# Stores of the experts' outputs in a two-block Trainium2 kernel: from one DMA a unit to one DMA a column block of four units

## The chip, the cores and the metric

The kernel runs on one core of one Trainium2 chip. The metric is the device time in microseconds (us) of one execution; the median of three runs of the kernel before is 2355.97 us (2354.79 to 2361.44).

The core has a matrix engine (PE, whose weight loads are listed as PEld), a vector engine (DVE), a scalar engine (ACT), GpSimd (POOL), and a sequencer without arithmetic (SP) that issues most DMAs. Sixteen DMA engines move data between the large memory (DRAM) and the on-chip memory of 128 partitions.

## The reference, cut to what matters

Two transformer-like blocks run on 1024 tokens of 1024 channels in float32. The first one ends in a mixture of experts, the part that the change touches: each token picks one of 4 groups and in it 2 of 8 experts, so there are 2048 assignments to 32 experts.

```
g_prob = softmax(h @ w_group + b_group);  p_g, g_idx = top_k(g_prob, 1)
top_v, top_i = top_k(logits of the experts in that group, 2)
gate = p_g * softmax(top_v);  expert_id = g_idx * 8 + top_i
def expert_block(args):
    xb, e = args
    a_, b_ = split(xb @ w13[e], 2)          # w13[e]: 1024 x 1024
    return (silu(a_) * b_) @ w2[e]          # w2[e]: 512 x 1024
out = segment_sum(ys * row_w[:, None], row_tok)
x = x + g2 * out
```

## The kernel before

The stages run one after the other: input projection and mixers of the first block, routing (`route`), the experts (`experts`, the stage "moe"), `middle` (adds the weighted expert outputs to x, then the second block's projection), attention, and a feed-forward part.

**Units and groups.** In `experts` the assignments are sorted by expert and cut into units of 32 tokens (TOK) of one expert. There are 80 of them, and four (CT) make a group of 128 rows, so 20 groups. An expert has between one and ten units.

**Weights.** An expert's weights are six pairs of 1 MB (two tiles of 128 rows by 1024). SP loads them by DMA into a ring of 17 places, `raw` (named moew_raw in the profile, L1607). A load into a place waits until the last unit of the expert that held it has copied it (`s_copied`), and until the load before with the same pair number has landed. For every unit DVE and ACT copy its expert's pairs from the ring into the working tiles: `wup`, which uses the memory of x (x_res in the profile, L1570), and `wdown` (L1581). So an expert with three units is loaded once and copied three times.

**A unit's computation.** PE computes `up` (L1673): 32 tokens as weights, four blocks of the expert's columns in four quarters of the array, into `hu`. ACT applies silu (L1714), DVE multiplies by the other half (L1768), PE transposes the result (`turn_a`, L1662), ACT copies it (L1718), and PE computes `down` (L1684) into `yp`. There partition 32 j + t holds token t of the unit and column block j of 256 columns. PE runs `down` of a unit after `up` of the next one, with `turn_a` in the middle of that `up`.

**The output.** DVE copies `yp` to `ysb` (`y_out`, L1773), a slice of acc_sq by the unit's place u in its group. ACT stores it to `y_scratch` in DRAM (`send`, L1722). Both happen two units late: at step u the output of unit u-2. A slice is written again one group later, after its store has landed (`s_sent`). The routing's row numbers `slots` let `middle` gather the outputs by token (L1851).

**Tokens.** For each group GpSimd gathers 128 token rows into `xg`, PE transposes them (L1656), and ACT and DVE write them, scaled, to `xt` (L1594, L1592).

**What sets the order.** It is written out by hand: each engine's program has a body `group` of four steps, one for each u, in a loop. Within an engine everything runs in that order; between engines semaphores count. At the end of the stage SP loads x back from `xt_scratch` (L1622), ACT waits for all stores, and all engines meet before `middle` starts.

Of the kernel before, what the change touches and what calls it, by code (L numbers as in the profile page):

```python
# [21 lines left out]
P = 128  # L22
T = 1024
D = 1024
KT = D // P
# [12 lines left out]
TOK = 32  # L38
CT = P // TOK
# [5 lines left out]
FW, YW = FF // CT, D // CT  # L45
# [218 lines left out]
class Kernel:  # L264
# [1268 lines left out]
    def experts(self):  # L1533
# [7 lines left out]
        with self.stage("moe") as st:  # L1541
            wup, wdown = self.x, st.sb("wdown", [P, FF // P, D])
            xg, idx, s_idx, s_g = self.xg, self.idx, self.s_idx, self.s_g
            xt = st.sb("xt", [P, KT, P])
            act_, at = st.sb("act", [P, FW]), st.sb("at", [P, KC, P])
            ysb = self.acc_sq[:, :].rearrange("p (u c) -> p u c", u=CT)
            hu = [st.ps(f"hu{b}", [P, HALF]) for b in range(2)]
            yp = [st.ps(f"y{b}", [P, HALF]) for b in range(2)]
            xturn, aturn = st.ps("xturn", [P, D]), st.ps("aturn", [P, HALF])
            s_copied = [st.sem(f"copied{p}") for p in range(NPAIR)]  # L1550
            s_upfree, s_downfree = st.sem("up_free"), st.sem("down_free")
            s_silu, s_act, s_aturn, s_at, s_yout = (st.sem(n) for n in ("silu", "act", "aturn", "at", "yout"))
            s_sent = [st.sem(f"sent{b}") for b in range(CT)]
            s_xturn = st.sem("xturn")
            s_xt = {k: st.sem("xt_" + k) for k in ("act", "dve")}
            ngroups = lambda e: e.value_load(self.groups[0:1, 0:1], min_val=0, max_val=NGRP - 1)
# [4 lines left out]
            rows = lambda j: slice(TOK * j, TOK * (j + 1))  # L1561

            def copy_up(e, k, v, pieces, o, then=lambda: None):

                for n_, (t, n) in enumerate(pieces):
                    e.wait_ge(s_w[t // 2], 16 * o + 16)
                    e.wait_ge(s_upfree, KT * v + (t + n))
                    e.nop(nofuse=True)
                    to, src = flat(wup, t, n), landed(o, t, n)
                    m = e.activation(to, src, ACT.Copy) if k == "act" else e.tensor_copy(to, src)  # L1570
                    m.then_inc(s_copied[t // 2], n)
                    if n_ == 0:
                        then()

            def copy_down(e, k, v, o):
                t, n = DOWN[k]
                e.wait_ge(s_w[t // 2], 16 * o + 16)
                e.wait_ge(s_downfree, FF // P * v + (t - KT + n))
                e.nop(nofuse=True)
                to, src = flat(wdown, t - KT, n), landed(o, t, n)  # L1580
                m = e.activation(to, src, ACT.Copy) if k == "act" else e.tensor_copy(to, src)  # L1581
                m.then_inc(s_copied[t // 2], n)
# [14 lines left out]
            with st.block() as blk:  # L1597
# [107 lines left out]
                @blk.scalar  # L1705
                def _(e):
                    n = ngroups(e)
                    e.preload_act_table(ACT.Silu)
                    for b in range(CT):
                        e.sem_inc(s_sent[b], 16)  # L1710

                    def silu(v, u):
                        e.wait_ge(s_upfree, KT * v + 2 * KT)
                        e.activation(act_[:, :], hu[u % 2][:, 0:FW], ACT.Silu).then_inc(s_silu, 1)  # L1714

                    def copy_a(v):
                        e.wait_ge(s_aturn, v + 1)
                        e.activation(at[:, :, :].rearrange("p c t -> p (c t)"), aturn[:, 0:FW], ACT.Copy).then_inc(s_at, 1)  # L1718

                    def send(v, u):  # L1720
                        e.wait_ge(s_yout, v + 3)
                        e.dma_start(self.y_dram[bass.ds(TOK * v, TOK), :].rearrange("t (j c) -> j t c", j=CT), ysb[:, u, :]).then_inc(s_sent[u], 16)  # L1722
                    def group(g, unit, first=False):
                        x = {} if first else {-1: expert(e, unit(-1))}
                        for u in range(CT):
                            if u or not first:
                                silu(unit(u - 1), (u - 1) % CT)
                                if LATE_ACT[u % 2]:
                                    copy_up(e, "act", unit(u), LATE_ACT[u % 2], x[u])
                                copy_down(e, "act", unit(u - 1), x[u - 1])  # L1730
                            if u == 0:
                                x[1] = expert(e, unit(u + 1))
                            if u or not first:
                                copy_a(unit(u - 1))

                            def more():
                                if u == 0:
                                    x[0] = expert(e, unit(u))
                                if u < CT - 1:
                                    x[u + 2] = expert(e, unit(u + 2))  # L1740
                            copy_up(e, "act", unit(u + 1), UP_ACT, x[u + 1], more)
                            if u == CT - 1:
                                copy_x(e, "act", g + 1)
                            if u >= 2 or not first:
                                send(unit(u - 2), (u - 2) % CT)
                    copy_up(e, "act", 0, UP_ACT, expert(e, 0))
                    copy_x(e, "act", 0)
                    group(0, lambda u: u, True)
                    with e.Fori(0, NGRP - 1) as i:
                        with e.If(i < n):  # L1750
                            group(i + 1, lambda u: CT * i + (CT + u))
                    silu(CT * n + (CT - 1), CT - 1)
                    copy_down(e, "act", CT * n + (CT - 1), expert(e, CT * n + (CT - 1)))
                    copy_a(CT * n + (CT - 1))
                    send(CT * n + (CT - 2), CT - 2)
                    send(CT * n + (CT - 1), CT - 1)
                    for b in range(CT):
                        e.wait_ge(s_sent[b], 16 * n + 32)
                    e.nop(nofuse=True)

                @blk.vector
                def _(e):
                    n = ngroups(e)
                    e.sem_inc(s_yout, 2)

                    def gated(v, u):
                        e.wait_ge(s_silu, v + 1)
                        e.tensor_tensor(act_[:, :], act_[:, :], hu[u % 2][:, FW:2 * FW], ALU.mult).then_inc(s_act, 1)  # L1768

                    def y_out(v, u, sent):  # L1770
                        e.wait_ge(s_downfree, FF // P * v + 2 * (FF // P))
                        e.wait_ge(s_sent[u], 16 * sent)
                        e.tensor_copy(ysb[:, u, :], yp[u % 2][:, 0:YW]).then_inc(s_yout, 1)  # L1773
                    def group(g, unit, first=False):
                        x = {} if first else {-1: expert(e, unit(-1))}
                        for u in range(CT):
                            if u or not first:
                                gated(unit(u - 1), (u - 1) % CT)
                                copy_down(e, "dve", unit(u - 1), x[u - 1])
                            if u == 0:  # L1780
                                x[1] = expert(e, unit(u + 1))
                            if u >= 2 or not first:
                                y_out(unit(u - 2), (u - 2) % CT, g + 1 if u >= 2 else g)

                            def more():
                                if u == 0:
                                    x[0] = expert(e, unit(u))
                                if u < CT - 1:
                                    x[u + 2] = expert(e, unit(u + 2))
                            copy_up(e, "dve", unit(u + 1), UP_DVE[(u + 1) % 2], x[u + 1], more)  # L1790
                            if u == CT - 1:
                                copy_x(e, "dve", g + 1)
                    copy_up(e, "dve", 0, UP_DVE[0], expert(e, 0))
                    copy_x(e, "dve", 0)
                    group(0, lambda u: u, True)
                    with e.Fori(0, NGRP - 1) as i:
                        with e.If(i < n):
                            group(i + 1, lambda u: CT * i + (CT + u))
                    gated(CT * n + (CT - 1), CT - 1)
                    copy_down(e, "dve", CT * n + (CT - 1), expert(e, CT * n + (CT - 1)))  # L1800
                    y_out(CT * n + (CT - 2), CT - 2, n + 1)
                    y_out(CT * n + (CT - 1), CT - 1, n + 1)


    def middle(self):
# [822 lines left out]
```

## Time and profile before

| | |
|---|---|
| median of 3 runs | 2355.97 us |
| span of the profiled execution (the page gives no other time for it) | 2356.3 us |
| PE busy | 2145.3 us, 91% |
| DVE, ACT, POOL busy | 1237.3, 823.3, 564.1 us |
| DMA bytes, mean rate over the span | 370.12 MB, 157 GB/s |
| weight loads of the experts | 192 of 1024 KB |
| stores of the experts' outputs | 80 of 128 KB |

An engine's busy time is the sum of its instructions; PE's matmuls are pipelined, so a busy PE need not be at its peak. The experts' stage lies between about 522 and 1189 us. "ACTq" and "SPq" are the sequencers of these engines: a row with them is the issue of a DMA, not its transfer. Of the transfer itself the views give the number of packets, the bytes, and the time that the packets took as a share of sixteen engines.

### The profile page before, as it was taken

Reading aid. Unit: us, or ns where it says so; the run is one execution under the profiler, and the core shown is the slowest. Engines: PE = TensorE matmul, PEld = TensorE weight load, DVE = VectorE, ACT = ScalarE, POOL = GpSimd, SP = SyncE. Lnnn points to the kernel's source line nnn. Section 1 sums busy time; section 2 is a strip of 40 time slices with the busy share of each in tenths; the row PEclk is TensorE's granted clock in tenths of the full one; section 3 lists DMA queues with packets and bytes.
Section 4 is the critical chain, followed back from the end, with each engine's and each line's share of the span. In section 5 each row is a group of like instructions: output and inputs, shape, how many; then the busy total and the mean of one; then the engine's idle time right before and its main releaser. Section 6 shows DMA issues by size and latency. Waiting matters only on the chain. (4 is left out here: it accounts for less than half of the span.)

```text
span 2356.3 us, 43499 instructions
## 1 busy us (share of the span) xinstructions
PE 2145.3 (91%) x15936; PEld 1602.9 (68%) x15936; DVE 1237.3 (53%) x1539; ACT 823.3 (35%) x1198; POOL 564.1 (24%) x379
## 2 busy tenths in 40 slices
PE   5999988995787997878779989899999999999998
PEld 4788766783444554434458867688888888888887
DVE  7888356425676886757746458534332123212244
ACT  5122165113566885756622038512100001000023
POOL 1433211310000000000025632123323323233243
PEclk9999999996898998988869999999999999999999
DMA  7633042329999699999752300111111111111113
GB/s 276 245 126 118 28 161 66 134 90 409 410 360 333 242 380 353 355 356 354 293 194 90 95 26 1 34 47 45 45 53 45 47 51 45 54 45 52 47 56 123
DMA packets 104883, 370.12 MB, mean 157 GB/s; under 512 B 7948, under 2 KB 19052, under 8 KB 104428
## 3 DMA queue, kind: packets, MB, share of 16 engines
q1 hardware_dynamic: 86476, 326.68, 38.7%
q10 hardware_dynamic: 13008, 23.07, 2.6%
q0 software_dynamic: 5328, 19.40, 2.2%
q8 instruction: 47, 0.77, 0.1%
q14 instruction: 24, 0.20, 0.0%
HBM read 337.61 MB, written 31.51 MB: 157 GB/s over the span
## 5 line engine op out<-in xcount | busy, mean ns | idle before, releaser
L1673 PE MATMUL moe_hu<-x_res,moe_xt 128*32 128x256 f32 x5120 | 338.0, 407 | 63.6 <-DVE moe_xt L1592 24.1
L1570 DVE COPY x_res<-moew_raw 128x2048 f32 x243 | 270.4, 1135 | 171.4 <-DMA moew_raw<-in_w 106.0
L1673 PEld LDWEIGHTS moe_hu<-x_res,moe_xt 128*32 128x32 f32 x5120 | 162.5, 115 | 194.9 <-issue 58.7
L244 PE MATMUL ff_acc<-ff_yh,ff_w_hi 128*128 128x512 f32 x704 | 274.4, 390 | 0.0
L244 PE MATMUL ff_acc<-ff_yl,ff_w_hi 128*128 128x512 f32 x704 | 273.9, 389 | 0.0
L244 PE MATMUL ff_acc<-ff_yh,ff_w_lo 128*128 128x512 f32 x704 | 273.9, 389 | 0.0
L1570 ACT ACTIVATE x_res<-moew_raw 128x2048 f32 (+1 forms) x121 | 197.7, 1634 | 97.8 <-DMA moew_raw<-in_w 69.6
L212 POOL CAST ff_w_hi<-ff_w_raw 128x1024 fp32r<-128x1024 f32 (+1 forms) x82 | 81.9, 998 | 547.1 <-PE ff_acc L244 547.1
L244 PE MATMUL ff_acc<-xh,ff_w_hi 128*128 128x512 f32 x480 | 188.2, 392 | 3.3 <-DVE ff_w_lo L228 2.6
L214 POOL TENSOR_TENSOR ff_w_lo<-ff_w_raw,ff_w_hi 128x1024 fp32r<-128x1024 f32 (+1 forms) x82 | 188.6, 2300 | 6.6
L244 PE MATMUL ff_acc<-xl,ff_w_hi 128*128 128x512 f32 x480 | 187.3, 390 | 0.0
L244 PE MATMUL ff_acc<-xh,ff_w_lo 128*128 128x512 f32 x480 | 187.3, 390 | 0.0
L1581 ACT ACTIVATE moe_wdown<-moew_raw 128x2048 f32 x80 | 153.2, 1915 | 29.3 <-PE moe_y L1684 23.9
L1684 PE MATMUL moe_y<-moe_wdown,moe_at 128*32 128x256 f32 x2560 | 158.0, 389 | 2.4 <-ACT moe_at L1718 2.4
L2430 ACT ACTIVATE ff_gs<-ff_gs 128x1024 f32<-128x1024 f32 x22 | 23.3, 1061 | 379.7 <-DVE ff_gs L2490 379.7
L244 PEld LDWEIGHTS ff_acc<-ff_yh,ff_w_hi 128*128 128x128 f32 x704 | 132.2, 188 | 28.3 <-DVE ff_yl L2479 0.5
L244 PEld LDWEIGHTS ff_acc<-ff_yh,ff_w_lo 128*128 128x128 f32 x704 | 132.2, 188 | 27.7
L244 PEld LDWEIGHTS ff_acc<-ff_yl,ff_w_hi 128*128 128x128 f32 x704 | 132.2, 188 | 27.3 <-issue 0.2
L1630 POOL COPY moew_idx<-rows 128x1 int32 (+1 forms) x20 | 10.6, 529 | 540.3 <-PE moe_xturn L1656 540.3
L244 PE MATMUL in_acc<-xh_mix,in_w_hi 128*128 128x512 f32 x336 | 132.1, 393 | 1.9 <-POOL in_w_lo L214 1.6
L244 PE MATMUL in_acc<-xh_mix,in_w_lo 128*128 128x512 f32 x336 | 130.8, 389 | 0.0
L244 PE MATMUL in_acc<-xl_mix,in_w_hi 128*128 128x512 f32 x336 | 130.8, 389 | 0.0
(426 smaller groups left out, 3734.4 us busy)
## 6 DMA issues: line engine op xcount, KB each, us to landing
moew_raw<-in_w SPq DMA_DIRECT2D x192, 1024.0 KB
ff_w_raw<-in_w_up SPq DMA_DIRECT2D x44, 512.0 KB, 3.5
mid_w_raw<-in_w_qkv SPq DMA_DIRECT2D x24, 512.0 KB
in_w_raw<-in_w_in SPq DMA_DIRECT2D x23, 512.0 KB, 3.6
xbc<-in_w_ada SPq DMA_DIRECT2D x20, 512.0 KB, 7.9
y_scratch<-acc_sq ACTq DMA_DIRECT2D x80, 128.0 KB
ff_w_raw<-in_w_down SPq DMA_DIRECT2D x16, 512.0 KB, 3.6
x_res<-in_w_ada SPq DMA_DIRECT2D x14, 512.0 KB, 4.1
```

The costliest lines, as they stand in the source:

```text
L212: pool.tensor_copy(hi, raw).then_inc(self.s_hi, 1)
L214: pool.tensor_tensor(lo, raw, hi.bitcast(F32), ALU.subtract).then_inc(self.s_split, 1)
L244: m = pe.matmul(o, w[:, b, k * P:(k + 1) * P], x[:, k, h:h + HALF], start=(k == 0 and t == 0), stop=(k == kt - 1 and t == 2))
L1570: m = e.activation(to, src, ACT.Copy) if k == "act" else e.tensor_copy(to, src)
L1581: m = e.activation(to, src, ACT.Copy) if k == "act" else e.tensor_copy(to, src)
L1630: e.tensor_copy(idx[:, :], self.rows[:, g:g + 1] if isinstance(g, int) else self.rows[:, bass.ds(g, 1)]).then_inc(s_idx, 1)
L1673: m = e.matmul(hu[u % 2][rows(j), 0:2 * FW].rearrange("p (a f) -> p a f", a=2), xt[:, t, rows(u)], w[:, :, FW * j:FW * (j + 1)], start=(t ...
L1684: m = e.matmul(yp[u % 2][rows(j), 0:YW], at[:, t % KC, rows(t // KC)], wdown[:, t, YW * j:YW * (j + 1)], start=(t == 0), stop=(t == FF // ...
L2430: st.act(e.activation(gs[:, :], gs[:, :], ACT.Silu), f"silu{n}")
```

## The change

The outputs of a whole group are collected and stored by column block. `ysb` becomes a tensor of its own with two buffers, one for even and one for odd groups. When all four units of a group are copied, ACT issues four DMAs, one for each column block j. Each one reads the 32 partitions of block j with the four units' 256 columns, and writes 32 tokens x 4 units x 256 columns, with the tokens as the outer dimension. DVE's copy addresses the buffer by a register and waits, at the first unit of a group, until the stores of two groups before have landed. A store of block j waits for the one before of the same block. `xt` moves into the memory of acc_sq.

```diff
-            xt = st.sb("xt", [P, KT, P])
+            xt = self.acc_sq[:, :].rearrange("p (k t) -> p k t", k=KT)
-            ysb = self.acc_sq[:, :].rearrange("p (u c) -> p u c", u=CT)
+            ysb = st.sb("ysb", [P, 2, CT, YW])
...
-                    for b in range(CT):
-                        e.sem_inc(s_sent[b], 16)
+                    for j in range(CT):
+                        e.sem_inc(s_sent[j], 32)
...
-                    def send(v, u):
-                        e.wait_ge(s_yout, v + 3)
-                        e.dma_start(self.y_dram[bass.ds(TOK * v, TOK), :].rearrange("t (j c) -> j t c", j=CT), ysb[:, u, :]).then_inc(s_sent[u], 16)
+                    def send(g, j):
+                        e.wait_ge(s_yout, CT * g + (CT + 2))
+                        e.wait_ge(s_sent[j], 16 * g + 32)
+                        e.nop(nofuse=True)
+                        src = ysb[rows(j), bass.ds(g % 2, 1), :, :].rearrange("t o u c -> t (o u) c")
+                        dst = self.y_dram[bass.ds(P * g, P), YW * j:YW * (j + 1)].rearrange("(u t) c -> t u c", u=CT)
+                        e.dma_start(dst, src).then_inc(s_sent[j], 16)
...
-                            if u >= 2 or not first:
-                                send(unit(u - 2), (u - 2) % CT)
+                            if not first:
+                                for j in ((), (0,), (1, 2), (3,))[u]:
+                                    send(g - 1, j)
...
-                    send(CT * n + (CT - 2), CT - 2)
-                    send(CT * n + (CT - 1), CT - 1)
-                    for b in range(CT):
-                        e.wait_ge(s_sent[b], 16 * n + 32)
+                    for j in range(CT):
+                        send(n, j)
+                    for j in range(CT):
+                        e.wait_ge(s_sent[j], 16 * n + 48)
...
-                    def y_out(v, u, sent):
+                    def y_out(v, u, g):
                         e.wait_ge(s_downfree, FF // P * v + 2 * (FF // P))
-                        e.wait_ge(s_sent[u], 16 * sent)
-                        e.tensor_copy(ysb[:, u, :], yp[u % 2][:, 0:YW]).then_inc(s_yout, 1)
+                        if u == 0:
+                            for j in range(CT):
+                                e.wait_ge(s_sent[j], 16 * g + 16)
+                        e.nop(nofuse=True)
+                        b = g % 2 if isinstance(g, int) else bass.ds(g % 2, 1)
+                        to = ysb[:, b, u, :] if isinstance(g, int) else ysb[:, b, u, :].rearrange("p o c -> p (o c)")
+                        e.tensor_copy(to, yp[u % 2][:, 0:YW]).then_inc(s_yout, 1)
...
-                                y_out(unit(u - 2), (u - 2) % CT, g + 1 if u >= 2 else g)
+                                y_out(unit(u - 2), (u - 2) % CT, g if u >= 2 else g - 1)
```

In ACT's loop over groups, here around the ends of the steps u=1 and u=2, the stores stand just ahead of the silu of the next unit (L1714; ISA and REGISTER_ALU are the sequencer's waits and arithmetic):

```order
 L1722 ISA
-L1722 DMA y_scratch<-acc_sq 4x32x256
+L1726 ISA
+L1726 REGISTER_ALU
+L1726 DMA y_scratch<-moe_ysb 32x4x256
 L1713 REGISTER_ALU
 L1714 ACTIVATE moe_act<-moe_hu 128x128
...
-L1722 ISA
-L1722 DMA y_scratch<-acc_sq 4x32x256
+L1726 ISA
+L1726 DMA y_scratch<-moe_ysb 32x4x256
+L1726 ISA
+L1726 DMA y_scratch<-moe_ysb 32x4x256
```

The pattern of a store turns from 4x32x256 to 32x4x256. Two stand at the end of step u=2, one each at u=1 and u=3, none at u=0. After the loop, once the last unit is computed, ACT's program ends so:

```order
-L1721 REGISTER_ALU
-L1722 ISA
-L1722 DMA y_scratch<-acc_sq 4x32x256
-L1758 ISA
+L1726 ISA
+L1726 REGISTER_ALU
+L1726 DMA y_scratch<-moe_ysb 32x4x256
+L1726 ISA
+L1726 DMA y_scratch<-moe_ysb 32x4x256
+L1726 ISA
```

Four stores follow the last output copy, where one did.

## Rows read from the trace of the kernel before

**Rows 1.** The page, part 1: busy us (share) xinstructions of each engine.

```profile
PE 2145.3 (91%) x15936; PEld 1602.9 (68%) x15936; DVE 1237.3 (53%) x1539; ACT 823.3 (35%) x1198; POOL 564.1 (24%) x379
```

**Rows 2.** Stretches: us, busy of PE, PEld, DVE, ACT, POOL, PE clock, DMA share, GB/s.

```profile
600.00:625.00 25.00, 20.81 (x339) 11.54 (x331) 15.60 (x22) 13.48 (x17) 1.37 (x2) 0.97 1.03 409
...
650.00:675.00 25.00, 24.56 (x420) 13.85 (x416) 22.06 (x29) 21.41 (x23) 1.55 (x2) 1.00 1.02 391
675.00:700.00 25.00, 16.87 (x230) 8.09 (x222) 12.82 (x18) 11.24 (x14) 0.96 (x2) 0.80 0.97 324
...
775.00:800.00 25.00, 24.57 (x413) 13.67 (x409) 22.06 (x31) 21.42 (x23) 1.55 (x2) 1.00 0.45 160
...
875.00:900.00 25.00, 21.78 (x337) 11.74 (x327) 15.25 (x22) 15.13 (x18) 1.56 (x2) 0.93 0.94 333
...
591.00:754.00 163.00, 129.06 (x1944) 68.53 (x1948) 107.58 (x141) 102.68 (x111) 6.66 (x10) 0.86 1.00 376
754.00:870.00 116.00, 113.81 (x1907) 64.04 (x1903) 100.92 (x135) 98.64 (x108) 7.79 (x10) 1.00 0.78 300
870.00:1165.00 295.00, 242.12 (x3701) 127.81 (x3691) 197.09 (x258) 189.60 (x202) 13.98 (x18) 0.88 0.96 348
```

**Rows 3.** Waits in 870:1165: us in total, times, longest.

```profile
DVE x_res L1570 <- DMA moew_raw<-in_w: 62.5, 19, 7.3
...
ACT x_res L1570 <- DMA moew_raw<-in_w: 31.6, 7, 8.7
```

**Rows 4.** DMA in 875:900: GB/s by 0.625 us; queue: packets, MB, share.

```profile
GB/s 369 192 300 356 441 424 210 198 315 396 426 379 154 375 424 413 379 213 346 349 346 411 401 410 354 344 411 401 333 97 138 298 410 423 426 210 116 310 413 424
...
q10 hardware_dynamic: 489, 0.48, 5.5%
```

**Rows 5.** DMA in 522:1166: packets and MB, and issues.

```profile
DMA packets 66462, 226.46 MB, mean 352 GB/s; under 512 B 3844, under 2 KB 13674, under 8 KB 66451
...
moew_raw<-in_w SPq DMA_DIRECT2D x192, 1024.0 KB
y_scratch<-acc_sq ACTq DMA_DIRECT2D x77, 128.0 KB
```

**Rows 6.** Stores in 591:754: duration of the issue ns min/median/max, first and last start.

```profile
L1722 ACTq DMA_DIRECT2D y_scratch<-acc_sq x21: 560/1047/1178, 591.0 to 753.1; - x21
L1722 ACTq MOVE y_scratch<-acc_sq x19: 29/34/38, 608.1 to 753.0; - x19
...
L1722 ACTq DMA_DIRECT2D y_scratch<-acc_sq x20: 564/1047/1057, 753.1 to 868.1; - x20
...
L1722 ACTq DMA_DIRECT2D y_scratch<-acc_sq x40: 554/1047/1057, 874.8 to 1182.6; - x40
```

**Rows 7.** Timeline in 762:768: start us, us, engine, line, operation [idle before].

```profile
762.65 0.29 DVE L1768 TENSOR_TENSOR moe_act<-moe_act,moe_hu 128x128 f32<-128x128 f32 x1 [0.45 <-ACT moe_act L1714]
...
764.32 0.33 PE L1662 MATMUL moe_aturn<-consts,moe_act 128*128 128x128 f32 x1
...
766.49 1.05 ACTq L1722 DMA_DIRECT2D y_scratch<-acc_sq  x1
767.66 0.28 ACT L1714 ACTIVATE moe_act<-moe_hu 128x128 f32<-128x128 f32 x1 [0.68 <-issue]
```

**Rows 8.** Issues of h_scratch's stores (ns), and the reload of x (us to landing).

```profile
L1379 ACTq DMA_DIRECT2D h_scratch<-moew_raw x8: 334/335/384, 527.6 to 538.6; - x8
...
x_res<-xt_scratch SPq DMA_DIRECT2D x1, 4096.0 KB, 13.5
```

**Rows 9.** Timeline at the end of the stage, 1182:1190.

```profile
1181.96 0.42 DVE L1773 COPY acc_sq<-moe_y 128x256 f32<-128x256 f32 x1 [3.91 <-PE moe_y L1684]
1182.57 0.55 ACTq L1722 DMA_DIRECT2D y_scratch<-acc_sq  x1
1189.49 0.83 SPq L220 DMA_DIRECT2D mid_w_raw<-in_w_qkv  x2
```

**Rows 10.** DMA in 600:625: packets, MB, share of 16 engines.

```profile
q10 hardware_dynamic: 398, 0.40, 4.5%
```

More of the change, by code:

```diff
@@ L1552, in experts @@
             s_silu, s_act, s_aturn, s_at, s_yout = (st.sem(n) for n in ("silu", "act", "aturn", "at", "yout"))
-            s_sent = [st.sem(f"sent{b}") for b in range(CT)]
+            s_sent = [st.sem(f"sent{j}") for j in range(CT)]
             s_xturn = st.sem("xturn")
@@ L1800, in _ @@
                     copy_down(e, "dve", CT * n + (CT - 1), expert(e, CT * n + (CT - 1)))
-                    y_out(CT * n + (CT - 2), CT - 2, n + 1)
-                    y_out(CT * n + (CT - 1), CT - 1, n + 1)
+                    y_out(CT * n + (CT - 2), CT - 2, n)
+                    y_out(CT * n + (CT - 1), CT - 1, n)
     def middle(self):
```

## The prediction

> **What bounds the kernel now.** I read the views in this order: the busy times of the whole span and of the experts' stage by stretches, the DMA queues in the same stretches, the waits, and the timeline where a store is issued. [rows 1] shows TensorE (PE) busy for 91% of the span, and the reader might stop there. The diff touches only the experts' stage, from the first load at 522 us to the last at about 1166 us, and there the balance is another. [rows 2] has two kinds of stretches. In 650:675 and 775:800 PE is busy for 24.56 or 24.57 of 25 us: it is the bound there, and at 775:800 the loads even pause (160 GB/s), since the ring of 17 places is full. In 675:700 and 875:900 PE is busy for 16.87 and 21.78 us, and [rows 3] names what it misses: DVE and ACT wait for moew_raw, the landed weights, 62.5 + 31.6 us in 870:1165. So outside the middle stretch 754:870 the loads set the pace.
>
> How fast can loads be? In 600:625 everything together moved 409 GB/s; in those two stretches, with the loads waited for, 324 and 333. [rows 4] holds the clue: inside 875:900 the rate swings between about 420 GB/s and dips of 97, 116, 138 and 154 in slices of 0.625 us. A quarter of 410 is 102. Something regularly leaves about four of the sixteen DMA engines running alone, and twelve without work. The candidate is the store of y. [rows 5] counts 192 loads of 1024 KB and 77 stores in 522:1166. The store's pattern in the program is 4x32x256: four column blocks outermost. If it is cut over the engines by its outer dimension, four engines carry it. The loads are cut over all sixteen, and a load counts as landed only when its last share has landed, so all wait for those four.
>
> Does the size fit? In 875:900 the q10 packets (only y stores there) number 489 and took 5.5% of 16 x 25 us, 22 us: 45 ns each [rows 4]. A store is 128 KB in pieces of 1 KB, so 128 packets, 5.8 us of one engine's time: 1.44 us on each of four engines, 0.36 us on each of sixteen. Account for the four engines over 522:1166, 644 us [rows 5]: all bytes but the y stores are 226.46 - 77 x 0.131 = 216.4 MB, at 410 GB/s 528 us on every engine; 77 x 1.44 = 111 us more on the four. That is 639 of 644 us: the four are full nearly all the time, the other twelve would need only 528. If the stores were spread evenly already, the sum would be 528 + 28 = 556 us and 88 us of the stretch would be unexplained.
>
> The Trainium skill, "DMA: Bandwidth & Descriptors", section "Why a DMA increments its semaphore by 16 and not by 1", says that the number of engines of such a DMA is the largest number up to 16 that divides the slowest dimension of both patterns. By that rule it is 4 before and 16 after (32 tokens outermost); the trace agrees in its dips to a quarter.
>
> **The change part by part.**
>
> *The store's pattern, 4x32x256 to 32x4x256.* The number of stores stays 80 (four a group, 20 groups), and so do their 128 KB and their pieces of 1 KB. What changes is 1.44 - 0.36 = 1.08 us on each of the four engines per store. Where it is worth something: [rows 6] counts 21 stores in 591:754, 20 in 754:870 and 40 later. In the middle stretch PE is busy for 113.81 of 116 us [rows 2], so nothing is gained there; a faster load only fills the ring sooner. In the other two 61 stores give 61 x 1.08 = 66 us. PE must be able to follow: in the middle stretch a unit takes 116 / 20 = 5.8 us; 58 units in 591:754 and 870:1165 need 58 x 5.8 = 336 us, and the stretches would shrink from 458 to about 395. On the average there is room. In 650:675 and at times later PE is at its bound for a large expert, but the ring holds almost three experts, which evens this out. Bounds: 0 if nothing is spread, 80 x 1.08 = 86 us if it counts everywhere. I take 66, because rows 2 show only one long stretch where PE alone decides. Cover that goes: the wait for loads is next followed by PE itself, and in the stretch 754:870 the ring will be full for longer.
>
> *Send moved from one a unit to 0, 1, 2, 1 in a group.* An issue takes ACT's sequencer 1047 ns in the median, 554 ns at least [rows 6]. The number is the same, but at u=2 (u is the unit's place in its group) two follow each other, and behind them stands the silu of the next unit, for which DVE's gating and PE's transpose of act wait. [rows 7] shows the case in the PE-bound stretch: the issue of 1.05 us from 766.49 lets silu start only at 767.66, 0.68 us late. What hides a second one: the gated product of the unit before ended at 762.65 + 0.29 = 762.94, and its transpose came at 764.32, since PE was still in the first half of the next up. That is 1.38 us of cover, against at most 1.05 us more. So I cost it 0; with the cover gone it is 1.05 x 20 = 21 us. No row has this pattern from ACT. The nearest are 334 ns for h_scratch's stores on ACT [rows 8], which are 128 rows of 4 KB, and the present 1047 ns; if spreading brings it to the former, ACT gains up to 0.7 us a send, in a place where it costs little. I take the present duration. The order of the two sends and the stores before moves nothing on SP or GpSimd.
>
> *The waits.* A send waits for the output copy of the group's last unit, which DVE makes at u=1 of the next group ahead of the weight copies; ACT's former send at u=1 waited for the same copy. It waits also for the same block's store of the group before, issued a whole group (116 / 5 = 23 us) earlier. DVE's output copy waits at u=0 for all four stores of two groups before. None of these can be the last to come as long as a store lands within some 20 us; even the 4 MB reload of x, 32 times a store, lands in 13.5 us [rows 8]. Behind a late output copy PE's down would stand, so this is the place to look if it goes wrong. Cost 0.
>
> *Address arithmetic and the other buffer.* DVE's output copy gets a register address: one more sequencer instruction a unit. A MOVE of the sequencer costs 29 to 38 ns [rows 6], so 80 x 0.035 = 3 us if nothing covers it, and DVE is busy for only 22.06 of 25 us even when PE is the bound; 0 taken. xt moves into acc_sq and the outputs into a tensor of their own: same shapes, same engines, 0.
>
> *The end of the stage.* Before, one store is left after the last output copy: issued at 1182.57 us, and the next stage starts at 1189.49 [rows 9]. In the 6.9 us between lies the rest of the reload of x, 4 MB, which SP issues once the last `up` is done and which takes 13.5 us to land [rows 8]. Now all four stores are issued after that copy: three more issues of 0.55 to 1.05 us, 1.7 to 3.2 us, less about 1 us because each is spread. +2 us.
>
> The sum, on the profiled span of 2356.3 us: -66 + 0 + 0 + 0 + 2 = 2292.3. The page gives no other time of that execution, and its span stands 0.3 us above the median of the three runs (2355.97), so I forecast 2292.
>
> **The rivals.**
> 1. *PE takes over more of it.* If the ring does not even out the large experts, the gain is lost wherever PE is at its bound outside the middle. For it speaks 650:675 [rows 2]; four of the 18 such windows outside the middle have the same 24.56 us of PE, about a fifth. Against it stand the 17 places. Then the gain is 61 x 1.08 x 0.8 = 53 us, and with half of the 21 us for the double sends, 2356.3 - 53 + 2 + 10 = 2315.
> 2. *The rate has another ceiling.* If mixed reads and stores of 1 KB run at some 350 GB/s however they are cut, the new pattern gives nothing: 2356.3 + 2 = 2358. Against it: 409 GB/s in 600:625, with 398 such store packets in that window [rows 10], and the dips to a quarter. The Trainium skill, "DMA: Bandwidth & Descriptors", section "Specifications", gives a limit of about 358 GB/s of HBM for each core; by that rule this rival holds; the trace disagrees, with 409.
> 3. *It doesn't spread.* If the cut over the engines follows something else than the outer dimension (the four pieces of a partition, say), four engines keep the work: 2358 again.
> 4. *ACT becomes the bound: slower.* Its place is u=2 in a PE-bound group, its price the issue. In 754:870 ACT is busy for 98.64 of 116 us, 17.4 us free over five groups, 3.5 us a group, in which its four sends of 1.05 us lie, partly under a running activation (in rows 7 ACT idles for 0.68 of 1.05 us). If an issue of the new pattern took 2.1 us instead, that is 4.2 us more a group; with no cover 84 us over 20 groups: 2356.3 - 66 + 84 + 2 = 2376. It outweighs the gain from 66 / 80 = 0.8 us more an issue, so from about 1.9 us each. Nothing like that is in the rows of ACT's stores, 1178 ns is the longest [rows 6].
>
> **How the numbers follow.** The forecast has a chance of 0.65 (its own range 2280 to 2302), rival 1 0.21, rival 2 0.03, rival 3 0.04, rival 4 0.03; 0.04 is left for a larger gain (all 80 stores count, 2270, and cheaper issues). The range runs from 2268 (the full 86 us, and 4 us from cheaper issues) to 2325 (rival 1 with the whole 21 us of the double sends); what it leaves out is rivals 2 to 4 and little else. A difference under 0.3%, 7 us, can't be told from none. Faster by more: 0.65 + 0.21 + 0.04 = 0.90; within 0.3%: rivals 2 and 3, 0.07; slower: rival 4, 0.03.
>
> **What would show it.** Right: the total rate stays near 400 GB/s in the loads' stretches and its dips to about 100 go; DVE and ACT wait for moew_raw far less; the loads in the middle pause for longer at full ring; a group takes about 24 us in the PE-bound stretch as before; the stage ends near 1124. Wrong: issues of y_scratch well over 1.05 us, a silu that starts over 1.4 us late at u=2 and a PE idle before the transpose of act, or rates that stay at 350 with even slices.

## The result and the profile after

The changed kernel takes 2285.66 us (median of 4 runs, 2283.65 to 2288.01); the kernel before, in 4 runs, 2356.74 us. The ratio is 0.9691 (95% interval 0.9673 to 0.9710), 71 us less. The forecast was 2292 us, the range 2268 to 2325. The profiled execution has a span of 2286.2 us, against 2356.3.

First the experts' stage by stretches, which answer to [rows 2]. The last three are cut near the places where the same units end, not exactly there (the second of them holds 1976 matmuls, the middle stretch of before 1907). Columns: us, busy of PE, PEld, DVE, ACT and POOL, PE clock, DMA share, GB/s.

```profile
650.00:675.00 25.00, 24.56 (x420) 13.84 (x413) 22.05 (x31) 20.41 (x23) 1.55 (x2) 1.00 1.03 412
675.00:700.00 25.00, 22.07 (x374) 12.28 (x365) 19.30 (x26) 19.78 (x22) 1.41 (x2) 1.00 1.03 412
750.00:775.00 25.00, 24.56 (x420) 13.85 (x416) 22.06 (x31) 20.77 (x24) 1.56 (x2) 1.00 0.24 71
775.00:800.00 25.00, 24.56 (x420) 13.85 (x416) 21.74 (x29) 21.40 (x23) 1.56 (x2) 1.00 1.02 405
591.00:739.00 148.00, 130.17 (x2076) 71.56 (x2068) 110.38 (x147) 104.81 (x115) 6.45 (x10) 0.93 1.03 410
739.00:859.00 120.00, 117.80 (x1976) 66.27 (x1972) 105.27 (x139) 101.77 (x111) 7.80 (x10) 1.00 0.85 332
859.00:1105.00 246.00, 227.08 (x3657) 124.72 (x3649) 196.04 (x260) 188.30 (x205) 14.04 (x18) 0.96 1.01 406
```

In 675:700, where the loads were waited for, the rate is now 412 GB/s instead of 324. The pause at full ring has become deeper in one window (71 GB/s in 750:775) but is over in the next (405 in 775:800), where before two windows ran at 211 and 160. PE is busy for more of the time on both sides of the middle: 130 of 148 us where it was 129 of 163, and 227 of 246 where it was 242 of 295. Its granted clock rose there too, from 0.86 to 0.93 and from 0.88 to 0.96 of full speed.

The rate inside one stretch (40 slices of 0.625 us) and the queues, as in [rows 4]:

```profile
GB/s 413 400 413 406 413 385 423 418 419 419 420 419 400 406 387 410 421 413 424 390 419 419 419 420 419 419 374 403 436 413 426 406 413 387 413 419 419 419 413 406
...
q10 hardware_dynamic: 576, 0.52, 6.1%
```

The dips to a quarter are gone; the lowest slice has 374. The waits for landed weights in the kernel before (591:1165) and after (591:1105), us in total, times, longest:

```profile
DVE x_res L1570 <- DMA moew_raw<-in_w: 104.0, 34, 7.3
ACT x_res L1570 <- DMA moew_raw<-in_w: 65.6, 14, 9.5
```

```profile
DVE x_res L1570 <- DMA moew_raw<-in_w: 47.9, 20, 5.2
...
ACT x_res L1570 <- DMA moew_raw<-in_w: 28.0, 9, 5.4
```

They have more than halved. The output copies tell when a unit is through. These are three parts of the stage, before and then after, with the number of copies, duration in ns (min/median/max), and first and last start:

```profile
L1773 DVE COPY acc_sq<-moe_y x22: 414/416/419, 586.2 to 756.1; 128x256 f32<-128x256 f32 x22
...
L1773 DVE COPY acc_sq<-moe_y x20: 414/416/418, 764.2 to 878.5; 128x256 f32<-128x256 f32 x20
...
L1773 DVE COPY acc_sq<-moe_y x38: 414/416/425, 885.9 to 1182.0; 128x256 f32<-128x256 f32 x38
```

```profile
L1783 DVE COPY moe_ysb<-moe_y x22: 416/417/419, 590.1 to 738.4; 128x256 f32 x20, 128x256 f32<-128x256 f32 x2
...
L1783 DVE COPY moe_ysb<-moe_y x20: 414/417/418, 746.2 to 859.0; 128x256 f32 x20
...
L1783 DVE COPY moe_ysb<-moe_y x38: 414/417/425, 866.8 to 1113.6; 128x256 f32 x38
```

From the first copy to the 22nd it took 169.9 us and takes 148.3 (21.6 less); from there to the 42nd 122.4 and 120.6 (1.8 less); from there to the last 303.5 and 254.6 (48.9 less). Together 595.8 and 523.5, 72.3 less. In this profile the first copy starts 3.9 us later than before; with that and the end of the stage below, the sum is the 70 us between the two spans. The issues, and the end of the stage:

```profile
L1726 ACTq DMA_DIRECT2D y_scratch<-moe_ysb x80: 328/333/1288, 615.0 to 1117.2; - x80
...
DMA to landing us min/median/max: 2.0/5.9/7.6
```

```profile
1113.62 0.42 DVE L1783 COPY moe_ysb<-moe_y 128x256 f32 x1 [4.03 <-PE moe_y L1684]
1114.47 3.08 ACTq L1726 DMA_DIRECT2D y_scratch<-moe_ysb  x4
1119.78 0.83 SPq L220 DMA_DIRECT2D mid_w_raw<-in_w_qkv  x2
```

An issue takes 333 ns in the median, not 1047. From the start of the last output copy to the next stage it is 6.2 us, against 7.5 in [rows 9].

### The profile page after: what moved, and what is told of

Same layout as the page of the kernel before. It is cut to its first block and busy times, and to the rows that moved or that the text cites. A ratio compares the mean times of both kernels' runs of the same rounds, so it can differ in the third digit from the quotient of the medians.

```text
span 2286.2 us, 43740 instructions
## 1 busy us (share of the span) xinstructions
PE 2127.8 (93%) x15936; PEld 1600.1 (70%) x15936; DVE 1235.5 (54%) x1539; ACT 820.3 (36%) x1198; POOL 567.7 (25%) x379
## 3 DMA queue, kind: packets, MB, share of 16 engines
q10 hardware_dynamic: 13968, 23.07, 2.8%
## 5 line engine op out<-in xcount | busy, mean ns | idle before, releaser
L1673 PE MATMUL moe_hu<-x_res,acc_sq 128*32 128x256 f32 x5120 | 322.5, 394 | 27.1 <-DVE acc_sq L1592 14.4
L1570 DVE COPY x_res<-moew_raw 128x2048 f32 x243 | 269.6, 1135 | 110.5 <-PE moe_hu L1673 48.9
L1673 PEld LDWEIGHTS moe_hu<-x_res,acc_sq 128*32 128x32 f32 x5120 | 160.7, 113 | 146.9 <-issue 38.1
```

The lines of the kernel that those rows point to most:

```text
L1673: m = e.matmul(hu[u % 2][rows(j), 0:2 * FW].rearrange("p (a f) -> p a f", a=2), xt[:, t, rows(u)], w[:, :, FW * j:FW * (j + 1)], start=(t ...
```

## The experiments

All times are medians, with the kernel before (2357 to 2359 us) run beside them. Besides the time I use "the stage", from the start of the first output copy to that of the last: 595.8 us before, 523.5 after. The stage leaves out what happens ahead of it: the first load of the experts starts anywhere from 521.9 to 529.1 us in the profiles of these kernels, small_store aside.

**k16_alone: the pattern alone.** The kernel before with one line changed:

```diff
-    e.dma_start(self.y_dram[bass.ds(TOK * v, TOK), :].rearrange("t (j c) -> j t c", j=CT), ysb[:, u, :]).then_inc(s_sent[u], 16)
+    e.dma_start(self.y_dram[bass.ds(TOK * v, TOK), :].rearrange("t d -> (t d)").rearrange("(b a c) -> a b c", a=16, c=YW), ysb[:, u, :]).then_inc(s_sent[u], 16)
```

> The kernel before, with one thing changed: the 128 rows of a unit's store go to other places in the same 128 KB of DRAM, so that the pattern is 16x8x256 instead of 4x32x256. Stores stay one a unit from one buffer; the rows land in another order, so the output isn't the reference's. Theory (the four engines' load): all of the gain is there, 2287 us (2280 to 2295), issue of a store near 333 ns. Rival A (the gain is from grouping, later stores and two buffers): 2357. Rival B (both share): about 2320.

Measured: 2283.95 us, ratio 0.9687 (0.9674 to 0.9700); the stage 523 us. The whole gain is there with neither groups nor two buffers nor moved stores. Rival A falls. Its issues took 567 ns in the median, not the 333 that I had expected.

**grouped4: all but the pattern.** The changed kernel, each of the four stores one unit in the old pattern:

```diff
-    src = ysb[rows(j), bass.ds(g % 2, 1), :, :].rearrange("t o u c -> t (o u) c")
-    dst = self.y_dram[bass.ds(P * g, P), YW * j:YW * (j + 1)].rearrange("(u t) c -> t u c", u=CT)
+    src = ysb[:, bass.ds(g % 2, 1), j, :].rearrange("p o c -> p (o c)")
+    dst = self.y_dram[bass.ds(P * g + TOK * j, TOK), :].rearrange("t (a c) -> a t c", a=CT)
```

> The changed kernel with its groups, two buffers and positions of the stores, but each of a group's four stores takes one unit in the old pattern 4x32x256. Theory: as before the change, 2357 us (2350 to 2370), rates near 350 GB/s with dips to about 100. Rival A (grouping): 2286. Rival B: about 2320.

Measured: 2353.41 us, ratio 0.9981 (0.9972 to 0.9991), the stage 587.5 us. The rate in 875:900:

```profile
GB/s 420 411 408 419 406 415 413 419 418 413 413 411 408 415 403 426 411 387 405 413 408 429 411 400 396 429 408 243 126 280 339 387 387 259 208 395 395 387 370 372
```

The dip to 126 is back, and with it nearly all of the time. Grouping by itself is worth 5 us (2 to 7 by the interval); where these come from is open. The kernel also shows what the grouped stores do on four engines. DVE's output copy waits for earlier stores, 18.6 us in all and up to 3.3 us at once, and the middle part takes 125.8 us from the 22nd copy to the 42nd, where it took 122.4 before. And it shows two stores behind each other at the old pattern, here in the middle stretch:

```profile
774.92 1.92 ACTq L1726 DMA_DIRECT2D y_scratch<-moe_ysb  x2
776.96 0.28 ACT L1714 ACTIVATE moe_act<-moe_hu 128x128 f32<-128x128 f32 x1 [1.20 <-DMA y_scratch<-moe_ysb]
...
778.68 0.33 PE L1662 MATMUL moe_aturn<-consts,moe_act 128*128 128x128 f32 x1
```

The silu starts 1.20 us late, and PE's transpose still comes 5.58 us after the one before (773.10), as the ones of the two units ahead of it did (5.57 and 5.58 us).

**k8_alone and k2_alone: two more widths.** As k16_alone, with a=8 and a=2.

> As k16_alone, with the pattern 8x16x256 (rows in another order, output not the reference's). Theory: 5.8 / 8 = 0.72 us of each of eight engines a store, so 0.72 us less than before in the 61 stores outside the PE-bound stretch: 2357 - 44 = 2313 (2305 to 2320). Rival A: 2357. A rival by which only the order in DRAM matters gives the same time as k16_alone, 2287.

> As k16_alone, with the pattern 2x64x256 (rows in another order, output not the reference's). Theory: 2.9 us of each of two engines a store instead of 1.44, and with so long a queue the middle stretch counts too: 2357 + 80 x 1.44 = 2472 (2440 to 2480). Rival A: 2357. If only the issue's length mattered, 0.7 us or so more a store on ACT: about 2380.

Measured: 2304.65 us (ratio 0.9771, 0.9756 to 0.9786) and 2468.48 us (1.0477, 1.0461 to 1.0493). First the issues of k8_alone, then those of k2_alone and its rate in 875:900:

```profile
L1722 ACTq DMA_DIRECT2D y_scratch<-acc_sq x80: 616/1108/1244, 594.6 to 1133.7; - x80
```

```profile
L1722 ACTq DMA_DIRECT2D y_scratch<-acc_sq x80: 529/1746/16118, 591.2 to 1289.4; - x80
...
GB/s 429 416 413 419 423 418 411 429 419 416 410 403 410 413 403 419 419 406 426 413 239 125 49 49 56 56 52 49 49 49 49 49 49 49 46 49 49 48 48 82
```

With two engines the rate falls to 49 GB/s for some 11 us on end; two sixteenths of 410 are 51. With four it was a dip to about 100. The packets of queue q10 over the whole run tell the same, for k2_alone, before, k8_alone and k16_alone in this order:

```profile
q10 hardware_dynamic: 12848, 23.07, 2.5%
q10 hardware_dynamic: 13008, 23.07, 2.6%
q10 hardware_dynamic: 13328, 23.07, 2.7%
q10 hardware_dynamic: 13968, 23.07, 2.7%
```

At the same bytes the counts differ by 160, 320 and 640, which is 80 stores times 2, 4 and 8: a store has one packet more for each engine that it gains, if the engines are 2, 4, 8 and 16. The changed kernel has 13968 as well, so its 32 tokens outermost give 16; grouped4 has 13008. (A store before is thus 132 packets, 5.9 us of one engine at 45 ns, where the prediction took 128 and 5.8.) k8_alone shows another thing: its issues are as long as before (1108 ns), and it is still 54 us faster, 10 us more than I had expected. The rival by which only the order in DRAM matters, 2287 us, falls with it.

The stage against the store's time on each of its engines (5.76 us divided by their number) gives the price of that time:

| engines | us on each | stage, us | less than the row above | 80 stores' engine time less |
|---|---|---|---|---|
| 2 | 2.88 | 702.6 | | |
| 4 (before) | 1.44 | 595.8 | 106.8 | 115 |
| 8 | 0.72 | 543.2 | 52.6 | 58 |
| 16 (after) | 0.36 | 523.5 | 19.7 | 29 |

Down to eight engines nine tenths of it come back as time, in the last step two thirds. The first row is of another kind, though. In k2_alone DVE and ACT wait for landed weights for only 10.9 + 11.7 us; the two engines are full nearly all the time there too (an estimate as in the prediction: 528 + 80 x 2.88 = 758 us, against 767 us from the first load to the last output copy), but what waits for them is ACT, inside the issue of its stores (the last section has the rows).

**k16_busy: is it ACT's shorter issue?** In k16_alone an issue takes 567 ns, about 480 less than before. Here an idle ACT copy behind each store gives that back:

```diff
+    idle = [st.sb(f"idle{b}", [P, NEARLY]) for b in range(2)]
...
+    e.activation(idle[u % 2][:, :], self.consts[:, :], ACT.Copy)
```

> k16_alone (pattern 16x8x256, rows in another order, output not the reference's) with an ACT copy of 128x418 behind each store, about 0.6 us, which gives ACT back the time by which its issues became shorter (1047 to 333 ns). The copy's result is used by nobody. Theory (the DMA engines' load is the gain, ACT's time isn't): 2287 to 2297 us. Rival C (the shorter issues on ACT are the gain): 2340 to 2357.

Measured: 2283.19 us, ratio 0.9677 (0.9659 to 0.9695). Its issues and its idle copies:

```profile
L1723 ACTq DMA_DIRECT2D y_scratch<-acc_sq x80: 553/567/699, 593.2 to 1113.7; - x80
```

```profile
L1724 ACT ACTIVATE moe_idle<-consts x80: 532/552/563, 594.5 to 1114.3; 128x418 f32<-128x418 f32 x80
```

567 + 552 = 1119 ns of ACT a unit, and nothing lost. ACT's time at this place is no part of the gain.

**after_again and after_third** are the changed kernel beside others.

> The changed kernel once more, beside the next two on the same chip: 2286 us (2283 to 2289). It is what they are compared with.

Measured: 2283.88 us (ratio 0.9685, 0.9667 to 0.9702), and in the third set 2286.80 us (0.9693, 0.9676 to 0.9710).

**unit_blocks: the same relief without groups.** One store a unit becomes four of 32 x 256 (the counts of the semaphore, four times as large, are left out here):

```diff
-    e.dma_start(self.y_dram[bass.ds(TOK * v, TOK), :].rearrange("t (j c) -> j t c", j=CT), ysb[:, u, :]).then_inc(s_sent[u], 16)
+    for j in range(CT):
+        e.dma_start(self.y_dram[bass.ds(TOK * v, TOK), YW * j:YW * (j + 1)], ysb[rows(j), u, :]).then_inc(s_sent[u], 16)
...
```

> The kernel before, with its one store a unit cut into four DMAs of 32 rows of 1 KB, one for each column block; the output is the reference's. 320 stores of 32 KB, each spread over sixteen engines, from one buffer. Theory: the four engines are relieved as in the changed kernel, but ACT issues 4 x 333 = 1.33 us a unit instead of 1.05, in a place where some 1.4 us of cover stand: 2286 to 2300 us. If the issues bite in the PE-bound groups, up to 1 us a unit more: 2340. Rival A (grouping is the gain): 2357 or more.

Measured: 2289.47 us, ratio 0.9701 (0.9685 to 0.9718). It comes within 6 us of the changed kernel run beside it (0.9685), with one buffer and 320 issues. The middle part, where PE decides, takes 120.5 us in its trace, as in the other kernels with 8 or 16 engines (120.6). So this is what grouping is for: the spread pattern at a quarter of the issues. On this kernel that is worth 0.2%, about the limit of what these runs tell.

**small_store: what the spread stores still cost.** The first edit stores an eighth of the bytes; the second fills the rest of y_scratch with zeros in an earlier stage.

```diff
-    e.dma_start(self.y_dram[bass.ds(TOK * v, TOK), :].rearrange("t (j c) -> j t c", j=CT), ysb[:, u, :]).then_inc(s_sent[u], 16)
+    e.dma_start(self.y_dram[bass.ds(TOK * v, TOK // 2), 0:YW], ysb[0:TOK // 2, u, :]).then_inc(s_sent[u], 16)
...
-    with e.Fori(2 * T // P, NGRP) as i:
+    with e.Fori(0, NGRP) as i:
```

> The kernel before, whose stores of y carry an eighth: one column block of 16 tokens, 16x256, for each unit, 16 KB on sixteen engines. The rest of the outputs isn't stored, so the result isn't the reference's; y_scratch is filled with zeros by 16 more DMAs of 512 KB in the stage ssd, so the time is to be read in the experts' stage alone. It asks what the spread stores still cost there. If every engine's time counted, 80 x (0.36 - 0.05) = 25 us less from the first to the last output copy than after (524 us), 499. If PE has become the bound as far as the steps from 4 to 8 and from 8 to 16 engines suggest (54 of 58 us gained, then 21 of 29), about 12 us less, 510 to 515. If nothing of the stores is left on the path, 524.

Measured: the stage takes 507.8 us (608.9 to 1116.7), 15.7 less than after. (The time of the whole, 2290.84 us, carries the added fills.) Of 25 us of engine time 16 came back, where three profiles of the changed kernel differ by 2 us (523.5, 525.2, 523.2). So the loads still set part of the pace; 43.5 + 20.9 us of waits for landed weights are left.

**order_11 and order_11_again: an attempt at more.**

```diff
-    place = [r if r < EARLY else EARLY + (8 * (r - EARLY) + 7) % (NE - EARLY) for r in range(NE)]
+    place = [r if r < EARLY else EARLY + (11 * (r - EARLY) + 7) % (NE - EARLY) for r in range(NE)]
```

> The changed kernel with another order of the experts by rank (step 11 instead of 8 in the table that places them), the output is the reference's. PE pauses where several small experts follow each other and DMA where the ring is full; the new order has 5,3,2,1,4,2,1 units ahead of the one with ten. A queue model of the stage, fitted to the two profiles, gives 6 us less than after, 2278 us; a rival is that the order makes no difference, 2285 (2283 to 2288).

> order_11 once more, beside the changed kernel. If the 6.6 us that its experts' stage was shorter in the profile (517.0 after 523.6 us) are real, 2278 us, 6 less than after_third. If the time doesn't move by more than 2 us, something gives them back, and the profile's start of the stage (529.1 instead of 524.8 us for the first load) is the place to look.

Measured: 2284.52 us (ratio 0.9681, 0.9661 to 0.9701), then 2279.38 us (0.9664, 0.9648 to 0.9681) beside after_third's 2286.80. The stage is 517.0 us in the first profile and 521.1 in the second. Beside after_third, on the same chip, it is 7.4 us less, as expected; the first set had no changed kernel beside it, and there its time is that of the changed kernel elsewhere. The intervals overlap with those of the changed kernel. All ten runs of it have a median of 2282.5 us, the fourteen of the changed kernel 2285.1. That is the right sign, under half the size I expected; the order depends on how many tokens each expert gets here. I would not count it as shown.

## Why the prediction was right

*What bounds the stage* held: loads outside the middle part, held back by four engines. That was read from dips of the rate to a quarter and from the account of 639 of 644 us [rows 4, 5]. The two experiments that part pattern and grouping, the width 8, and the packet counts show it; the width 2 shows that a store keeps to few engines, while its time came mainly through ACT. Rivals 2 and 3 are refuted by the 412 GB/s after, and with rival 2 a ceiling near 350 GB/s for mixed traffic.

*The 66 us of the pattern* are the term that was a little too small: from the first output copy to the last it is 72 us. By parts: 21.6 measured for 21 stores x 1.08 = 23; 1.8 for 0; 48.9 for 40 x 1.08 = 43. The first two parts stand. The third part gained more than its own stores' engine time. What was left out is what the middle part hands on: I wrote that a faster load "only fills the ring sooner" there. A fuller ring at its end is a stock that the last part draws on. The traces show it: at the 22nd copy 77 loads have been issued in both kernels, at the 42nd 108 before and 111 after. Three loads of 1.05 MB at 410 GB/s are 7.7 us, and 6 are missing. Another source isn't excluded: PE's matmuls got shorter as its clock rose. In the last stretch 3701 of them took 242.1 us before, 65.4 ns each, and after it 3657 took 227.1 us, 62.1 ns each, 12 us less of PE's time. How much of that lay on the path no run tells. The clock goes with the waits here: before, it was 0.80 in 675:700, where PE was busy for 16.87 us, and 1.00 in 650:675 with 24.56 [rows 2].

*The pause* came out otherwise than the prediction's signs said: not longer, but shorter. Measured against 410 GB/s in windows of 5 us, some 27 us of loading are missing in 755:795 before, and some 21 us in 750:775 after. Between the 22nd and the 42nd copy 34 loads are issued, where it had been 31.

*PE takes over (rival 1)* is true in its kind and hardly in size. The steps of engine time came back to 93%, 91% and 68%, the first of them by another wait. The loss is there in the last step, but over the whole 72 of 86 us came, more than the 66 of the forecast and well over the 53 of the rival.

*The sends* were costed at 0 at the old 1047 ns, and the time agrees, but the duration was the wrong one of the two that I had bounded it with: it is the 333 ns of [rows 8]. With it rival 4 loses its ground. The 0 was right on its own account too, as far as it was tried: in grouped4 two stores in the old pattern take 1.92 us together, and PE's transpose isn't late. Two of 1.05 us with no shorter one among them stand in no run.

*The waits* cost 0 as costed: a store lands in 5.9 us in the median, and no wait of DVE or ACT in the stage after is for a store. That holds for spread stores; in grouped4 DVE waited for them for 18.6 us.

*The end of the stage* was forecast at +2 us and is -1.4 us (7.5 to 6.2): four issues take 3.08 us in all, and the stores land 2.0 to 3.2 us behind them. The runs part the two terms. With four sends in the old pattern this end takes 10.1 us (grouped4): 2.6 more than before, near what the three issues were costed at. With one send, spread, it takes 5.0 us (k16_alone): 2.5 less, and the prediction had given 1 us for that. With both it is 6.2. So the sign was wrong because the spread store's share was too small, and the size is small beside the gain.

## What to carry to other kernels

Look at the outer dimension of a small DMA before its size: here stores with under 5% of the stage's bytes set the pace of all large loads, since they sat on a quarter of the engines and the loads needed those too; spread, they left DVE and ACT less than half of their waits for landed weights. In the profile the sign was a rate that swung between full and k/16 of it (k engines), while the mean share of the DMA engines stayed high; the price was, down to eight engines, nine tenths of the store's time on each of its engines. A change of the pattern alone should be tried first; buffers and groups are needed only where the layout forces them.

## What the runs showed of the hardware that was not expected

- The issue of a store of 128 pieces of 1 KB on ACT takes, in the median, 1108 ns as 8x16x256, 1047 ns as 4x32x256, 567 ns as 16x8x256 and 333 ns as 32x4x256; as 32x256 (a quarter of the bytes) 322 ns. It doesn't follow the bytes, nor the number of engines alone (16 in the last three), and not the pattern alone either: 4x32x256 takes 0.56 us for one unit of each group and 1.05 us for the other three in 757:850, and 780 ns in the median in grouped4. What decides it is open.
- With two engines an issue took up to 16.1 us (median 1.7): ACT's sequencer was held inside the issue. In k2_alone the wait in front of silu that the profile files under "issue" is the largest of ACT, us in total, times, longest:

```profile
ACT moe_act L1714 <- issue: 230.1, 53, 15.3
DVE moe_act L1768 <- ACT moe_act L1714: 220.9, 44, 14.8
```

So the 107 us that two engines cost came mainly this way, with ACT, DVE and PE behind it standing still; the waits for landed weights are 23 us in that kernel, and 176 in the one before over the same window (560:1300).
- The mean DMA share showed 0.97 and 0.94 in stretches with 324 and 333 GB/s [rows 2], while DVE and ACT waited for loads. It adds up the packets' times, and these were longer than at full rate: in 675:700 the 1986 packets of q1 took 91.7% of sixteen engines, 185 ns each, and after the change 2393 took 91.6%, 153 ns each. Only slices as short as the dips show the idle engines: in 893:899, cut into slices of 0.15 us, the share reads 1 to 4 tenths where the rate is 68 to 130 GB/s.
